# Smaller first weight pieces, split constants and another order of the first products in a gated convolution layer

## What is computed

```
hn = rms_norm(h, norm_g[layer])
z = h @ w_in                       # here h is hn; 1024 x 3072
a, b, gate = jnp.split(z, 3, axis=-1)
u = a * jax.nn.sigmoid(b)
u = causal depthwise convolution of u with 31 taps + conv_b
uf = (uf - mu) * lax.rsqrt(var + LN_EPS) * ln_g + ln_b
u = jax.nn.silu(uf) * jax.nn.silu(gate)
h = h + u @ w_out
```

## Time and profile before

| what | value |
|---|---|
| median of 3 runs | 370.73 us |
| lowest and highest | 370.05 and 371.03 us |
| the profiled execution's own time | 370.11 us |
| its span | 368.0 us |
| TensorE busy in the span | 363.2 us (99%) |
| VectorE, GpSimd, ScalarE busy | 317.3, 273.8, 208.2 us |
| granted TensorE clock | full in every slice |
| TensorE's share of the chain that ended last | 97% |
| bytes moved | 39.33 MB |

### The profile page before, as it was taken

How to read it: one execution, slowest core, us unless ns; L and a number is a source line. 1 busy time by engine, 2 the same in 40 slices (tenths; PEclk the granted TensorE clock), 3 DMA queues, 4 the chain that set the end, 5 groups by cost and what they waited for, 6 DMA issues and landing times.

```text
span 368.0 us, 4866 instructions
## 1 busy us (share of the span) xinstructions
PE 363.2 (99%) x1632; PEld 296.3 (81%) x1632; DVE 317.3 (86%) x505; ACT 208.2 (57%) x317; POOL 273.8 (74%) x195
## 2 busy tenths in 40 slices
PE   7999999999999999999999999999999999999997
PEld 6888888888888888888888888888888888888886
DVE  4758799999999899998999999963789999996942
ACT  6979685568537632874666657643436971342400
POOL 0127999999999995999999999996676543458310
PEclk9999999999999999999999999999999999999999
DMA  7995011301111011111011110113313596064042
GB/s 268 399 406 190 19 57 57 113 4 57 57 59 57 2 59 57 57 59 38 19 61 57 57 55 5 57 59 110 118 59 115 183 391 226 2 229 172 30 161 97
DMA packets 13705, 39.33 MB, mean 107 GB/s; under 512 B 1520, under 2 KB 2032, under 8 KB 13680
## 3 DMA queue, kind: packets, MB, share of 16 engines
q1 hardware_dynamic: 13536, 38.87, 29.0%
q10 hardware_dynamic: 144, 0.15, 0.2%
HBM read 34.82 MB, written 4.19 MB: 106 GB/s over the span
## 4 chain that ended last, share of the span: by engine, by line
PE 97%; DMA 1%; SPq 0%; ACT 0%; DVE 0%; issue 0%
PE mm L580 67%; PE acc L675 12%; PE mm L675 9%; PE mm L597 6%; PE mm L648 2%; DMA nat<-x_t 1%; PE acc L666 0%; PE acc L656 0%; PE acc L574 0%; SPq L481 0%; ACT x_hi L745 0%; DVE nat L1196 0%; SPq L469 0%
## 5 line engine op out<-in xcount | busy, mean ns | idle before, releaser
L580 PE MATMUL mm<-x_hi,w_hi 128*128 128x512 f32 x352 | 139.9, 397 | 0.0
L580 PE MATMUL mm<-x_hi,w_lo 128*128 128x512 f32 x352 | 138.9, 395 | 0.0
L580 PE MATMUL mm<-x_lo,w_hi 128*128 128x512 f32 x352 | 138.8, 394 | 0.0
L1108 DVE SCALAR_TENSOR_TENSOR acc<-u,chan,acc 128x512 f32<-128x512 f32 x154 | 108.3, 748 | 0.1
L580 PEld LDWEIGHTS mm<-x_hi,w_lo 128*128 128x128 f32 x352 | 66.3, 188 | 15.4
L580 PEld LDWEIGHTS mm<-x_lo,w_hi 128*128 128x128 f32 x352 | 66.4, 189 | 15.0
L580 PEld LDWEIGHTS mm<-x_hi,w_hi 128*128 128x128 f32 x352 | 66.4, 189 | 14.9
L1408 POOL TENSOR_TENSOR pconv<-pconv,prod 128x512 f32<-128x512 f32 x60 | 76.8, 1302 | 0.0
L1108 DVE SCALAR_TENSOR_TENSOR acc<-u,w_sum,acc 128x512 f32<-128x512 f32 x90 | 67.3, 748 | 0.2
L834 ACT ACTIVATE prod<-u,chan 128x512 f32<-128x512 f32 x73 | 50.6, 718 | 16.0 <-POOL pconv L1408 12.8
L1352 POOL TENSOR_TENSOR w_lo<-raw,w_hi 128x1024 fp32r<-128x1024 f32 x21 | 50.6, 2410 | 8.1 <-ACT w_hi L784 8.0
(11 more groups left out here) (102 smaller groups left out, 526.0 us busy)
## 6 DMA issues: line engine op xcount, KB each, us to landing
raw<-w_in SPq DMA_DIRECT2D x22, 512.0 KB, 3.2
nat<-x_t SPq DMA_DIRECT2D x16, 256.0 KB, 5.9
sgate<-x SPq DMA_DIRECT2D x8, 512.0 KB, 11.3
raw<-w_out SPq DMA_DIRECT2D x8, 512.0 KB, 3.3
nat<-x SPq DMA_DIRECT2D x8, 512.0 KB, 9.1
y<-nat SPq DMA_DIRECT2D x15, 256.0 KB, 2.1
raw_late<-w_out SPq DMA_DIRECT2D x4, 512.0 KB, 3.8
sig<-w_out SPq DMA_DIRECT2D x4, 512.0 KB, 3.7
```

Source lines behind the costliest of these rows:

```text
L580: ins = nc.tensor.matmul(bank(("unit", m, h)), w[:, m % 3, k, :], xx[:, k, half(h)], start=(k == 0 and i == 0), stop=(k == KC - 1 and i == 2))
L1108: ins = nc.vector.scalar_tensor_tensor(dst, chain_in(j, chain, k), tap(j, chain, k), chain_bank(j, chain), ALU.mult, ALU.add)
```

## The change

The first weights come in six pieces instead of four: FIRST_PIECES now holds (unit, first k, end k), with pieces of 2, 2 and 4 blocks k for either unit, so two of 128 KB and one of 256 KB each. `PIECE` gives the piece of a (unit, k), for the waits of TensorE and SP. The second pieces of both units are loaded and split ahead of k = 2, the third ahead of 4 and 5. The constants are laid out with norm_g first. ScalarE's transfer at the start brings only norm_g (32 bytes a partition, semaphore `norm_in`); the rest (1,120 bytes a partition) is issued by SP ahead of the identity and counts `chan_in`. The splits of x wait for `norm_in`; VectorE waits for `chan_in` ahead of w_sum, ScalarE behind `split_w(4)` ahead of its first taps. FIRST_TERMS has the same twelve terms in another order.

```diff
-FIRST_PIECES = ((0, 0), (1, 0), (0, 1), (1, 1))
-PIECES_BEFORE = {0: (0,), 1: (1,), 4: (2,), 5: (3,)}
-FIRST_TERMS = ((0, 0, 0), (0, 0, 2), (1, 0, 0), (0, 0, 1), (1, 0, 1), (0, 1, 0), (1, 1, 0), (1, 0, 2),
-               (0, 1, 2), (1, 1, 2), (0, 1, 1), (1, 1, 1))
+FIRST_PIECES = ((0, 0, 2), (1, 0, 2), (0, 2, 4), (1, 2, 4), (0, 4, 8), (1, 4, 8))
+PIECE = {(m, k): i for i, (m, begin, end) in enumerate(FIRST_PIECES) for k in range(begin, end)}
+PIECES_BEFORE = {0: (0,), 1: (1,), 2: (2, 3), 4: (4,), 5: (5,)}
+FIRST_TERMS = ((0, 0, 0), (0, 0, 2), (1, 0, 0), (0, 0, 1), (1, 0, 1), (1, 0, 2),
+               (0, 1, 0), (0, 1, 2), (1, 1, 0), (1, 1, 2), (0, 1, 1), (1, 1, 1))
...
-        w_even = chan[:, 0:KC * HT].rearrange("p (j k) -> p j k", k=HT)
-        w_odd = chan[:, KC * HT:2 * KC * HT].rearrange("p (j k) -> p j k", k=HT)
-        conv_b, ln_g, ln_b, norm_g = (
-            chan[:, KC * (2 * HT + i):KC * (2 * HT + i + 1)] for i in range(4))
+        norm_g, conv_b, ln_g, ln_b = (chan[:, KC * i:KC * (i + 1)] for i in range(4))
+        w_even = chan[:, 4 * KC:KC * (4 + HT)].rearrange("p (j k) -> p j k", k=HT)
+        w_odd = chan[:, KC * (4 + HT):KC * (4 + 2 * HT)].rearrange("p (j k) -> p j k", k=HT)
...
+            sp.dma_start(chan[:, KC:], per_channel[:, KC:]).then_inc(chan_in, 16)
             sp.dma_start(ident[:], identity).then_inc(ident_in, 16)
...
                 if k == 5:
-                    sp.wait_ge(w_first_lo, 3)
+                    sp.wait_ge(w_first_lo, PIECE[0, KC - 1] + 1)
                     load_weights(2)
...
                 if t == 2:
-                    sp.wait_ge(w_first_lo, 4)
+                    sp.wait_ge(w_first_lo, PIECE[1, KC - 1] + 1)
                     load_weights(3)
...
-            act.dma_start(chan[:], per_channel).then_inc(chan_in, 16)
+            act.dma_start(chan[:, 0:KC], per_channel[:, 0:KC]).then_inc(norm_in, 16)
...
             split_first(0)
-            act.wait_ge(chan_in, 16)
+            act.wait_ge(norm_in, 16)
...
             split_w(4)
+            act.wait_ge(chan_in, 16)
             for n in range(2):
                 first_tap(n)
...
             split_first(0)
-            dve.wait_ge(chan_in, 16)
+            dve.wait_ge(norm_in, 16)
...
                 split_raw(1, k)
+            dve.wait_ge(chan_in, 16)
             nc.vector.tensor_tensor(w_sum[:], w_even, w_odd, ALU.add).then_inc(taps_ready, 1)
```

More of the change, by code:

```diff
@@ L186, in gated_conv_layer @@
         mm = ctx.enter_context(nc.psum_tensor("mm", [P, 4, HALF], F32))
+        norm_in = sem("norm_in")
         chan_in = sem("chan_in")
@@ L204, in gated_conv_layer @@
         rms_ready = sem("rms_ready")
-        w_first_in = [sem(f"w_first_in{i}") for i in range(4)]
+        w_first_in = [sem(f"w_first_in{i}") for i in range(len(FIRST_PIECES))]
         w_first_hi = sem("w_first_hi")
@@ L402, in rms_spread, with first_columns, first_ks @@
             return acc[:, 3 - h, :]
[L404 to L410, removed]
+        def first_columns(i):
+            _, begin, end = FIRST_PIECES[i]
+            return slice(begin * P, end * P)
+        def first_ks(i):
+            _, begin, end = FIRST_PIECES[i]
+            return slice(begin, end)
         def nth(kind, m):
@@ L585, in raw_term @@
             def raw_term(m, h, k, i):
-                piece = FIRST_PIECES.index((m, k // (KC // 2))) + 1
+                piece = PIECE[m, k] + 1
                 if i == 0:
@@ L748, in split_first @@
             def split_first(i):
-                m, part = FIRST_PIECES[i]
+                m = FIRST_PIECES[i][0]
                 act.wait_ge(w_first_in[i], 16)
-                nc.scalar.activation(w_hi[:, m, first_ks(part), :].rearrange("p k n -> p (k n)"),
-                                     raw[:, m, first_columns(part)], ACT.Copy).then_inc(w_first_hi, 1)
+                nc.scalar.activation(w_hi[:, m, first_ks(i), :].rearrange("p k n -> p (k n)"),
+                                     raw[:, m, first_columns(i)], ACT.Copy).then_inc(w_first_hi, 1)
             def rms_diagonal(t):
@@ L1032, in split_first @@
             def split_first(i):
-                m, part = FIRST_PIECES[i]
+                m = FIRST_PIECES[i][0]
                 dve.wait_ge(w_first_hi, i + 1)
-                nc.vector.tensor_tensor(w_lo[:, m, first_ks(part), :].rearrange("p k n -> p (k n)"),
-                                        raw[:, m, first_columns(part)],
-                                        w_hi[:, m, first_ks(part), :].rearrange("p k n -> p (k n)").bitcast(F32),
+                nc.vector.tensor_tensor(w_lo[:, m, first_ks(i), :].rearrange("p k n -> p (k n)"),
+                                        raw[:, m, first_columns(i)],
+                                        w_hi[:, m, first_ks(i), :].rearrange("p k n -> p (k n)").bitcast(F32),
                                         ALU.subtract).then_inc(w_first_lo, 1)
@@ L1485 @@
     per_channel = np.concatenate(
-        [taps(conv_w[0::2]), taps(conv_w[1::2])]
-        + [by_channel(arr(n)[0]) for n in ("a_conv_b", "a_ln_g", "a_ln_b", "norm_g")], axis=1)
+        [by_channel(arr(n)[0]) for n in ("norm_g", "a_conv_b", "a_ln_g", "a_ln_b")]
+        + [taps(conv_w[0::2]), taps(conv_w[1::2])], axis=1)
     arrays = {k: np.ascontiguousarray(v) for k, v in {
```

4 lines of the change are left out of this document (2 added, 2 removed).

## The result

| | before | changed |
|---|---|---|
| median | 370.5 us | 371.33 us |
| lowest and highest | 370.05 and 371.03 us | 370.97 and 372.55 us |
| the profiled execution's time and span | 370.11 and 368.0 us | 371.15 and 369.0 us |

These are 18 executions of each on one chip; the ratio is 1.0025 (95% interval 1.0018 to 1.0031). The changed kernel is 0.8 to 0.9 us slower. I had forecast 370.7, no change, and a range of 369.8 to 371.5. The time lies in the range, and within the 0.3% that I took for the limit of the measurement. But 18 executions of each tell 0.25% from nothing: the kernel is slower, and that my forecast did not have.

What follows compares the result with a forecast made beforehand. The prediction took TensorE's head as the bound, at most 1.55 us to win. Its 0.9 us lead would be waited off for unit 2's w_lo, itself 0.24 us later, so nothing won: 370.7 us, range 369.8 to 371.5.

Steps and rivals of the forecast that it cites:

- the prediction's own signs: Said to be wrong if unit 2 starts before 29.4 or after 30.3, or another wait appears behind it.
- d: Delay of the transfer stream up to columns (0,6): 0.24 us, from -0.06 to 0.75.
- What bounds the kernel: TensorE runs almost to the end after 7.63 us; only its head can win, at most 1.55 us.
- Less ahead of the first product: At the start, fewer bytes ahead of the first columns: TensorE starts at 5.05 for 5.74, gain 0.7 us.
- The first twelve products: TensorE's head: third x_hi split starts at 7.1 for about 7.5, giving TensorE a lead of 0.9 us.
- g: TensorE's lead from the 14th product on: 0.9 us, bounds 0.4 and 1.2.
- ScalarE and VectorE: Six splits for four add 0.42 us before column 4, absorbed ahead of columns (0,6); no wait for constants.
- SP: Three more issues put later loads 1.4 us later on SP; costs nothing, since the transfer queue is full.
- The stream up to columns (0,6): Transfers up to those columns: small pieces cost 0.14 us, 32-byte rows 0.1; delay 0.24 us in all.
- The sum: At unit 2, TensorE's 0.9 us lead is waited off for w_lo: start 29.82 for 29.80, nothing won.
- the stream slower: Rival: transfers ahead of columns (0,6) slow down; delay beyond 0.22 us reaches the end one for one; chance 0.08.
- The lead is kept: Rival: a better-filled stream brings unit 2's w_lo as early as TensorE; 369.8 us, chance 0.08.

Runs made afterwards that it cites:

- f2_halves: Kernel before, with the first 256 KB weight piece of each unit fetched as two 128 KB transfers of 64 partitions each; 372.56 us, ratio 1.0042.
- g3_extra: Kernel before, with two more 4 KB transfers (32-byte rows, into unused tiles) ahead of columns 2; 370.11 us, ratio 0.9986.
- f1_contig: Changed kernel, with each of its six weight pieces stored as a contiguous block in memory; 371.14 us, ratio 1.0011.
- h1_rows: g1_wide_contig, with its two early transfers as 256 rows of 1 KB instead of 128 rows of 2 KB; 370.31 us, ratio 0.9992.
- g4_after_vector_lo: Changed kernel, with unit 2's w_lo made by VectorE behind its last x_lo instead of by GpSimd; 371.40 us, ratio 1.0026.
- e1_const: Kernel before, with only the constants split: norm_g alone at the start, the rest from SP ahead of the identity; 370.26 us, ratio 0.9989.
- e2_pieces: Kernel before, with only the six weight pieces of 2, 2 and 4 blocks k; 370.83 us, ratio 0.9999.
- e4_wide: Changed kernel, with both units' early pieces side by side in memory, joined into 256 KB transfers with 2 KB rows, four transfers in all; 370.98 us, ratio 1.0011.
- g1_wide_contig: e4_wide, with each of its four transfers read from a contiguous block in memory; 369.98 us, ratio 0.9989.
- h2_best: g1_wide_contig, with unit 2's w_lo made by VectorE instead of GpSimd; 370.00 us, ratio 0.9989.
- f4_wide_early: e4_wide, with ScalarE splitting unit 2's weights between columns (0,5) and (0,6); 372.12 us, ratio 1.0039.

## Why the prediction was wrong

- **The outcome**: by the prediction's own signs it was wrong when unit 2 starts after 30.3, and it starts at 30.49. That 371.33 lies within the range is owed to the upper bounds of d and of the runs, not to the forecast of no change.
- **What bounds the kernel**: right. The head, and then TensorE without a gap; every profiled execution's time follows the start of unit 2.
- **Less ahead of the first product**: 5.05 forecast, 5.32 measured. The first piece landed 2.3 us after its issue, earlier than my 2.6 to 3.0, and the split of columns 0 started at 4.21, as forecast (4.2). But I had taken the warm-ups' end, 4.98, as fixed, and it is not. The tile `ones` in both traces (ns least, median, most; first and last start), first before, then changed:

```profile
L721 PE MATMUL acc<-ones x20: 274/421/582, 1.0 to 4.7; 128*128 128x128 f32 x20
```

```profile
L725 PE MATMUL acc<-ones x20: 421/422/580, 1.0 to 5.2; 128*128 128x128 f32 x20
```

  Before, the last warm-ups take 0.274 us, as all such products later; in the changed kernel all take 0.42, and the first weight loads of real products 0.33 us for 0.19. Loads of 0.33 us are those of the 1.2 GHz level, as f2_halves has them where its granted clock is 0.50. The profile shows 1.00 here, but the trace has no record of the granted clock yet: the first, of full clock, starts at 4.1 us before and at 6.6 in the changed kernel, and over all sixteen traces at 3.9 to 6.9 us, with the same warm-ups from 1.0 us on. So the first product can't start before 5.32 where the engine is slow; six traces have it at just that time. The Trainium skill ("TensorE: Matmul & The Clock Gate", What you observe) has this moment vary by 0.5 us either way from run to run; here the earliest and the latest lie 3.0 us apart. It cost the changed kernel 0.3 us at the first product and nothing at the 13th, which waited for x.
- **The first twelve products**: this step failed. "By the bytes it starts at 7.1": the columns 2 landed at 8.6. I had divided the bytes ahead of them by 400 GB/s, which the earlier trace rows show only from 14 us on, where all transfers are large. Among the small pieces the stream ran at 263 GB/s from 5 to 8 us, and even before the change at 356. g was -0.64 for +0.9, outside my bounds of 0.4 to 1.2.
- **ScalarE and VectorE**: right. The 256-column splits took 0.42 us; w_sum and the first taps waited for nothing.
- **SP**: right up to columns 2, where g3_extra's two more issues cost nothing; for the columns behind, which came 0.9 us late in its trace, it isn't settled.
- **The stream up to columns (0,6)**: this term was mis-sized, 0.24 (up to 0.75) for 0.98, and for 1.42 up to columns (0,3). I had costed the small pieces by their rows (47.8 us of engine time per MB for 1 KB rows, 43.5 for 2 KB). What costs is the transfer of 128 KB: 52 us per MB in the changed kernel and 62 in f1_contig, for 45 in h1_rows, which has rows of 1 KB too. Even the 2 KB rows of x take longer there: one occupied an engine for 89 ns from 5 to 8 us before, for 97 in the changed kernel and 124 in f1_contig. In the changed kernel engines are also idle, share 0.76 from 6 to 7 us, for which the sum had no term behind the first 2 us. "How well the engines fill in the first 2 us is not seen: 0.2 us either way" was the right doubt with the wrong bound and the wrong place: most of the loss lay between 3 and 8 us. The other term of d, 0.1 for the 32-byte rows of norm_g, was about right: in the changed kernel its 144 packets took 1.3% of 16 engines x 6 us, 0.08 us.
- **The sum**: the mechanism held. My formula gives unit 2 at 29.58 + d, with d = 0.98 that is 30.56; it was 30.49. There the cap and the head fall together: TensorE was 0.68 late by itself, and g4_after_vector_lo, which has no such cap, is no earlier. The cap itself is seen in e1_const, e2_pieces, e4_wide, f1_contig, g1_wide_contig, g3_extra and h1_rows, whose weight load of unit 2 waits 0.30 to 0.51 us for w_lo. What the sum lacked is a head that comes late: g entered with +0.4 to +1.2 only.
- **The Trainium skill** ("DMA: Bandwidth & Descriptors", Anatomy of one DMA) has a fit, made on transfers issued by GpSimd, by which I estimated 0.3 us won by halving a piece. Of the first transfer that is borne out: with the constants out of its way, 256 KB land 2.7 us after their issue in e1_const and 128 KB 2.3 to 2.4 in the changed kernel and g4_after_vector_lo; the rest of the step from 3.3 is the constants'. Of the stream behind it the opposite was measured. Its advice to make transfers large (same page, Rules for kernel authors) was the better guide here.
- **The rivals**: the stream slower was what happened, by its mechanism, at 0.08. I had asked that d be 1.3 before it counted, because the rows gave 0.75 at most. But the 1 KB rows are the stores at the very end, in a queue that took 26% of the engines; no row had transfers of 128 KB among others in a full queue.
- **The lead is kept** did not happen in the changed kernel. In e1_const, where the stream stays whole, w_lo of unit 2 comes no earlier (it ends at 29.39 for 29.36), so what that kernel keeps is the slack of the forecast and not this rival; h2_best keeps its lead by another edit, w_lo on VectorE.

Open stay two things. Why the changed kernel's median is 0.5 us above that of e2_pieces, whose trace has the same head, so whether the small pieces cost their full price only together with the split constants or the new order; and why transfers of 128 KB cost the engines more per byte.

## To carry to other kernels

A rate read where transfers are large does not hold where they are made small: to bring one thing sooner, take other bytes out of its way (the constants: columns 2 0.5 us earlier in the trace) or join pieces that are needed together, in contiguous blocks (14th product at 8.91, for 9.16 with the constants alone), and don't halve the pieces, even where that brings the first one sooner. None of this measured more than 0.11% here, less than the 0.14% of g3_extra, which should gain nothing. Before pricing a lead, follow the chain that is late next, and let the head be late in the sum as well as early. Divide share by rate: it tells an idle engine from one that needs longer for its bytes. Work that is moved on one engine to relieve a chain has to be held against what then runs beside it on the engines that share a port.

## What was not expected of the hardware

- Rows of 2 KB that lie 8 KB apart in memory, in the first transfer of a program, cost 1.3 us: columns 0 land at 5.5 in e4_wide and f4_wide_early and at 4.1 to 4.2 in g1_wide_contig, h2_best and h1_rows.
- In every trace one fetch of instructions of 16 KB passes through the transfer engines between 19 and 23 us. It is one packet that occupies one engine for 1.0 to 1.1 us. The transfers in flight then come 0.2 to 1.6 us late (1.0 us in the trace of before, 0.55 in the changed kernel's). That it is the cause was not tested.
- TensorE fell back to the 1.2 GHz level within the program, from 9.0 to 12.4 us in f2_halves, after it had idled 0.73 and 1.12 us.
